# Dilated attention with paired heads on the two column halves, and a last product by token tiles, in a two-block decoder on one core

## What is computed

```python
# dilated attention, per query block and head slot h, groups g = 0..2 with their own keys
sc = q_g @ k_g.T * scale                    # masked to t - dil*j
p_g, den_g = exp(sc - m), sum(exp(sc - m))
o_g = (p_g @ v_g) / den_g
w = softmax over g of (m_g + log(den_g))    # so that sum_g w_g o_g = sum_g p_g v_g / sum_g den_g
y_a = sum_g(w_g * o_g) @ w_proj_a
mixed = sigmoid(gate_a) * y_a + sigmoid(gate_b) * y_b
x = x + mixed @ w_out

# end of the second block, last layer
y = square(relu(h @ w1)) @ w2
x = x + y * rsqrt(mean(y * y) + eps) * g[5]      # this x is the output
```

## Time and profile before

| | us |
|---|---|
| median of 3 runs | 1407.98 |
| the profiled execution's own time | 1406.7 |
| its span, first to last instruction | 1404.9 |
| TensorE busy | 1382.0 (98%) |
| VectorE busy | 1012.8 (72%) |
| ScalarE busy | 741.0 (53%) |
| POOL busy | 80.7 (6%) |
| mean granted TensorE clock | 0.998 |

### The profile page before, as it was taken

One profiled execution on the slowest core, in us unless ns is written; L12 is line 12 of the kernel. 1 busy time (PEld: TensorE's weight loads), 2 busy tenths in 40 slices (PEclk: granted clock), 3 DMA queues, 4 the chain that ended last, 5 costly groups with the idle time before them and its releaser, 6 DMA issues.

```text
span 1404.9 us, 20190 instructions
## 1 busy us (share of the span) xinstructions
PE 1382.0 (98%) x7868; PEld 1179.3 (84%) x7868; DVE 1012.8 (72%) x1529; ACT 741.0 (53%) x1136; POOL 80.7 (6%) x90
## 2 busy tenths in 40 slices
PE   8999999999999999999999999999999999999997
PEld 6899888888888997888888778888888878888886
DVE  5565678777764657977787776887676866886665
ACT  4564555455445554555555666654445664554443
POOL 0000001000000000211111001000000000100000
PEclk9999999999999999999999999999999999999999
DMA  9744355555565334656655424358866523355551
GB/s 304 242 139 151 121 180 195 195 180 182 178 209 180 121 120 153 219 191 206 208 198 159 152 90 132 124 195 225 218 191 207 168 88 117 115 191 197 192 198 71
DMA packets 154437, 242.31 MB, mean 172 GB/s; under 512 B 4523, under 2 KB 107067, under 8 KB 154078
## 3 DMA queue, kind: packets, MB, share of 16 engines
q1 hardware_dynamic: 150626, 227.23, 49.1%
q0 software_dynamic: 3712, 13.77, 3.6%
q10 hardware_dynamic: 4, 0.01, 0.0%
HBM read 239.03 MB, written 1.97 MB: 172 GB/s over the span
## 4 chain that ended last, share of the span: by engine, by line
PE 93%; DVE 4%; ACT 1%; issue 1%; DMA 0%; POOL 0%; SPq 0%; DVEq 0%; ACTq 0%
PE ps L953 19%; PE ps L919 17%; PE ps L926 16%; PE ps L923 16%; PE ps L956 10%; PE ps L1031 3%; PE ps L1119 3%; PE ps L1085 2%; PE ps L1100 1%; DVE wlo L2129 1%; PE ps L993 1%; PE ps L995 1%; PE ps L994 1%; DVE x L2563 0%; PE ps L1572 0%
## 5 line engine op out<-in xcount | busy, mean ns | idle before, releaser
L2129 DVE TENSOR_TENSOR wlo<-raw,whi 128x1024 fp32r<-128x1024 f32 (+1 forms) x432 | 538.6, 1258 | 197.2 <-ACT whi L1659 196.6
L1659 ACT CAST whi<-raw 128x1024 fp32r<-128x1024 f32 (+1 forms) x432 | 446.5, 1042 | 272.3 <-PE ps L926 174.3
L953 PE MATMUL ps<-act,whi 128*128 128x512 f32 x1184 | 324.9, 395 | 1.2 <-DVE wlo L2129 0.9
L919 PE MATMUL ps<-whi,mhi 128*128 128x512 f32 (+2 forms) x688 | 236.4, 393 | 1.9 <-DVE mlo L2156 1.9
L953 PEld LDWEIGHTS ps<-act,whi 128*128 128x128 f32 x1184 | 204.8, 189 | 31.9 <-DVE wlo L2129 1.6
L926 PE MATMUL ps<-whi,mlo 128*128 128x512 f32 (+2 forms) x688 | 231.4, 385 | 0.0
L923 PE MATMUL ps<-wlo,mhi 128*128 128x512 f32 (+2 forms) x688 | 231.1, 385 | 0.0
L956 PEld LDWEIGHTS ps<-act,wlo 128*128 128x128 f32 x1184 | 182.6, 189 | 25.7
L956 PE MATMUL ps<-act,wlo 128*128 128x256 f32 x1184 | 189.4, 281 | 0.0
L919 PE MATMUL ps<-whi,act 128*128 128x256 f32 (+1 forms) x512 | 169.2, 331 | 0.0
L923 PE MATMUL ps<-wlo,act 128*128 128x256 f32 (+1 forms) x512 | 165.2, 323 | 0.0
(11 more groups left out here) (269 smaller groups left out, 1471.8 us busy)
## 6 DMA issues: line engine op xcount, KB each, us to landing
raw<-in_mlp_w SPq DMA_DIRECT2D x64, 1024.0 KB, 5.3
raw<-in_w_up SPq DMA_DIRECT2D x44, 1024.0 KB, 5.1
raw<-in_w_in SPq DMA_DIRECT2D x39, 1024.0 KB, 5.1
raw<-in_w_down SPq DMA_DIRECT2D x22, 1024.0 KB, 4.9
raw<-in_ev_w_in SPq DMA_DIRECT2D x10, 1024.0 KB, 5.4
raw<-in_w_out SPq DMA_DIRECT2D x8, 1024.0 KB, 5.0
raw<-in_xa_wkv SPq DMA_DIRECT2D x4, 1024.0 KB, 5.3
raw<-in_ev_w_out SPq DMA_DIRECT2D x4, 1024.0 KB, 5.1
```

The lines of the kernel that those rows point to most:

```text
L919: nc.tensor.matmul(o, hi[:, kx, rows_], wh[:, k, c0:c0 + w], start=first and h == 0 and k == 0 and (tt == 0 or at[1] == 0), stop=False)
L953: nc.tensor.matmul(both, wh[:, k, w], act2[:, kx].rearrange("p i n -> p (i n)"), start=kx == 0, stop=False)
L1659: nc.scalar.copy(whi[:, m % HL, 0:w], raw[:, n % RAW, h * w:h * w + w]).then_inc(hi_done, 1)
L2129: nc.vector.tensor_tensor(wlo[:, m % HL, 0:w], raw[:, n % RAW, h * w:h * w + w], whi[:, m % HL, 0:w].bitcast(F32), ALU.subtract).then_inc( ...
```

## The change

For the dilated heads:

- `values` gives way to `column_values`: two units (heads h and h + 1 of one query tile) at a time; the values are stationary, 128x64, and the turned exponents move, 128 columns; the two heads write partitions 0 to 63 and 64 to 127 of bank 6, blocks of the two heads in turn. The result lies with head dimensions on the partitions and queries along the row, as the projection wants it. The values of a pair (j, j + 1) stand at step j + 4.
- The copy of a unit waits until the values of the pair before its own pair are done.
- The sums belong to queries, which now lie along the row. VectorE takes all 8 reciprocals at once, POOL spreads each over the 64 columns of its head (`spread_shares`), TensorE turns that (`turn_shares`, between the two halves of "pb"), ScalarE copies it to SBUF, and VectorE multiplies bank 6 by it. ScalarE takes the high half of the product and VectorE the low one, both from SBUF. The turning in the middle of "pb" is gone.
- In ScalarE's program the copy of the turned shares stands ahead of the sigmoids.

For the end: the last chunk is done by token tiles (`tile_chunk`), and squares, mean, root, gain and addition follow tile by tile; tile 0 is added in one operation of 128x1024 and stored at once, tile 1 in two halves, each stored when ready.

The operations are those of `column_values`, `turn_shares` and the copies first (the first `u0 + j - j % 2` stands in ScalarE's program and in the same form in VectorE's), then the two sequences at the end of the attention, then `tile_chunk` and `last_tiles` for the end.

```diff
+            def spread_shares(l):
+                pool.wait_ge(share_ready, l + 1)
+                nc.gpsimd.tensor_copy(spread.rearrange("p (t h d) -> p t h d", t=TT, h=HG), rden[:, :, 0:HG].unsqueeze(3).to_broadcast([P, TT, HG, HD])
+                                      ).then_inc(spread_ready, 1)
...
+                def column_values(i):
+
+                    pair = [(u0 + i + j, us[i + j]) for j in range(2)]
+                    for u, _ in pair:
+                        wait_copied(pe, u)
+                    n = len(us[i]["pv"])
+                    for b in range(n):
+                        for u, d in pair:
+                            row = half(d["slot"])
+                            mm = nc.tensor.matmul(ps[row:row + HD, d["o_bank"], d["o_col"]:d["o_col"] + P], d["pv"][b],
+                                                  values_of(u, d)[:, b * P:(b + 1) * P], start=b == 0, stop=b == n - 1)
+                    mm.then_inc(at_o, 2)
...
-                        if WIDE_LAG + 1 <= i:
-                            values(i - WIDE_LAG - 1)
+                        j = i - WIDE_LAG - 2
+                        if j >= 0 and j % 2 == 0:
+                            values(j)
...
+                def turn_shares():
+                    bank = group_bank(("y1", l, "a"))
+                    pe.wait_ge(spread_ready, l + 1)
+                    wait_copied(pe, first_unit["dil", l] + len(units_of["dil", l]) - 1)
+                    for b in range(2):
+                        for qt in range(TT):
+                            mm = nc.tensor.transpose(bank[:, SEQ * b + P * qt:SEQ * b + P * qt + P], spread[:, SEQ * qt + P * b:SEQ * qt + P * b + P], ident)
+                    mm.then_inc(pe_grp, 1)
...
-                                   middle=attended if h else None)
+                        half_chunk(plan.jobs["pb", l][0], h, mhi, mlo, 2, [[(0, 512, yb(tt, 0)), (512, 512, yb(tt, 1))] for tt in range(TT)], True, True)
+                        if h == 0:
+                            turn_shares()
...
-                pe.wait_ge(grp_dve, plan.by_number[plan.groups["y1", l, "a"]][2])
+                pe.wait_ge(attended_lo, l + 1)
...
-                            if u0 + j >= 2:
-                                act.wait_ge(at_o, u0 + j - 1)
+                            if u0 + j - j % 2:
+                                act.wait_ge(at_o, u0 + j - j % 2)
...
+                take(("y1", l, "a"), shares)
                 act.wait_ge(gate_pre, 2 * NGC * (l + 1))
                 for c0 in (D, 0):
                     nc.scalar.activation(gates[:, :, c0:c0 + D], gates[:, :, c0:c0 + D], ACT.Sigmoid).then_inc(gate_done, 1)
                 split_half(f0 + 2 * NGC + 4)
-                take(("y1", l, "a"), blocks(mhi, 0))
+                act.wait_ge(o_ready, o_counts["dil", l])
+                nc.scalar.copy(blocks(mhi, 0), attended).then_inc(attended_hi, 1)
...
+                    if after and i == len(units_of["dil", l]) + 1:
+                        dve.wait_ge(at_e, first_unit["dil", l] + len(units_of["dil", l]))
+                        nc.vector.reciprocal(rden[:, :, 0:HG], den[:, :, 0:HG]).then_inc(share_ready, 1)
                     if i % 2 == 0 and i:
                         gate_out(3 + i // 2)
                     split_half(f0 + 10 + i)
...
-                for qt in range(TT):
-                    norm_out(("dil", l), HG * qt, HG, heads_of(o_nat, qt, 0, HG), TT * HG)
+                dve.wait_ge(at_o, first_unit["dil", l] + len(units_of["dil", l]))
+                dve.wait_ge(grp_act, plan.by_number[plan.groups["y1", l, "a"]][1])
+                nc.vector.tensor_tensor(attended, ps[:, 6, :], shares, ALU.mult).then_inc(o_ready, 2)
...
                 gate_b(0, 0)
-                lo_of(("y1", l, "a"), mhi, mlo, 0)
+                dve.wait_ge(attended_hi, l + 1)
+                nc.vector.tensor_tensor(blocks(mlo, 0), attended, blocks(mhi, 0).bitcast(F32), ALU.subtract).then_inc(attended_lo, 1)
...
+            def tile_chunk(n, hi, lo, k0, bank):
+                for tt in range(TT):
+                    for c in range(2):
+                        o = ps[:, bank(tt, c), :]
+                        for h in range(2):
+            ...
+                            nc.tensor.matmul(o, xh, wh, start=False, stop=False)
+                            nc.tensor.matmul(o, xh, wl, start=False, stop=False)
+                            mm = nc.tensor.matmul(o, xl, wh, start=False, stop=h == 1)
...
+                gain(0, 0)
+                mean(0)
+                n = gain(0, 1)
+...
+                add(0, slice(0, D)).then_inc(x_ready, 1)
+                gain(1, 0)
+                mean(1)
+                n = gain(1, 1)
+...
+                for c in range(2):
+                    add(1, slice(512 * c, 512 * c + 512)).then_inc(x_ready, 1)
```

More of the change, by code:

```diff
@@ L657, in build_network @@
             rs_count[k] = total
+        attended, spread, shares = o_nat[:, 0, 0:512], o_nat[:, 1, 0:512], o_nat[:, 0, 512:1024]
         def sbk(h):
@@ L890, in _ @@
                             root((key, l), 2, True, ss[:, i, tt:tt + 1], rstd[:, i, tt:tt + 1])
+                    elif key == "ym" and l == DEPTH - 1:
+                        i = NORM[key, l]
+                        for tt in range(TT):
+                            root((key, l), 2, True, ss[:, i, tt:tt + 1], rstd[:, i, tt:tt + 1])
+                        break
                     else:
@@ L1132, in values_pair @@
                         values(i + 1)
-                return scores, turn_pair if not wide_units else turn, values_pair if not wide_units else values
+                return scores, turn_pair if not wide_units else turn, values_pair if not wide_units else column_values
             def attention(key, each=None):
@@ L1876, in _, with squares @@
                 split_half(n0 + 4)
-            def squares(job, key, l, banks=yb, cs=(0, 1)):
+            def squares(job, key, l, banks=yb, cs=(0, 1), tiles=range(TT)):
                 i = NORM[key, l]
                 for c in cs:
-                    for tt in range(TT):
+                    for tt in tiles:
                         product(job(c), tt, c)
@@ L2100, in _ @@
                     memory_hi(l + 1, n0)
-                squares(lambda c: ("w2", l, NMB - 1), "ym", l)
+                if l + 1 < DEPTH:
+                    squares(lambda c: ("w2", l, NMB - 1), "ym", l)
+                else:
+                    for tt in range(TT):
+                        squares(lambda c: ("w2", l, NMB - 1), "ym", l, tiles=(tt,))
         @block.vector
@@ L2582, in add_normed, with last_tiles, gain, mean @@
                 add(1)
+                dve.wait_ge(x_ready, x_count(key, l))
+            def last_tiles(key, l, job):
+                n_gain[0] += 1
+                n_sq[0] += 4
+                i = NORM[key, l]
+                dve.wait_ge(gainb_in, 16 * n_gain[0])
+                def gain(tt, c):
+                    product(job, tt, c)
+                    dve.wait_ge(ss_ready, n_sq[0] - 3 + 2 * tt + c)
+                    cs = slice(512 * c, 512 * c + 512)
+                    return mark(nc.vector.tensor_tensor(ystep[:, tt, cs], ps[:, yb(tt, c), :], gain_b[:, cs], ALU.mult))
+                def mean(tt):
+                    dve.wait_ge(ss_ready, n_sq[0] - 2 + 2 * tt)
+                    total = ss[:, i, tt:tt + 1]
+                    nc.vector.scalar_tensor_tensor(out=total, in0=total, scalar=EPS2, in1=ss[:, i, TT + tt:TT + tt + 1],
+                                                   op0=ALU.add, op1=ALU.add).then_inc(mean_ready, 1)
+                def add(tt, cs):
+                    return nc.vector.scalar_tensor_tensor(out=x[:, tt, cs], in0=ystep[:, tt, cs], scalar=rstd[:, i, tt:tt + 1],
+                                                          in1=x[:, tt, cs], op0=ALU.mult, op1=ALU.add)
+                gain(0, 0)
+                mean(0)
+                n = gain(0, 1)
+                dve.wait_ge(rstd_ready, rs_count[key, l])
+                after(n)
+                add(0, slice(0, D)).then_inc(x_ready, 1)
+                gain(1, 0)
+                mean(1)
+                n = gain(1, 1)
+                dve.wait_ge(rstd_ready, rs_count[key, l] + 1)
+                after(n)
+                for c in range(2):
+                    add(1, slice(512 * c, 512 * c + 512)).then_inc(x_ready, 1)
                 dve.wait_ge(x_ready, x_count(key, l))
```

49 lines of the change are left out of this document (36 added, 13 removed).

## The result

| | before | after |
|---|---|---|
| median, us | 1407.74 (6 runs, 1406.99 to 1407.98) | 1413.89 (6 runs, 1410.99 to 1415.03) |
| after / before | | 1.0039, 95% interval 1.0028 to 1.0050 |
| profiled execution, us | 1406.7 | 1412.05 |
| its span, us | 1404.9 | 1410.2 |
| mean granted TensorE clock | 0.998 | 0.997 |

The change makes the kernel slower by 0.4%. The forecast was 1410.2 with the range 1406.0 to 1414.0: the time lies in the range, at its upper end. (The mean counts the idle end of the program too: the 0.998 of before is nothing but its end, where the clock falls behind the last product.)

The account below looks back on a forecast made before the run. TensorE, busy for 98% of the span, was taken as the bound. Two layers at +2.2 us less 2.2 at the end gave +2.2 on 1406.7, 1408.9; the median being 1.3 higher, 1410.2, range 1406.0 to 1414.0.

Parts of the forecast that it names:

- part 1: Dilated attention, values in pairs on column halves: 2.0 us saved per layer up to the mark, bounds 1.7 to 2.3.
- the mark: Moment in the dilated attention where the turning of the seventh unit ends; "pa" started 10.7 us behind it before.
- part 2: From the mark to the turned shares: a bare VectorE copy, shares turned 6.7 to 7.4 us behind the mark, 7.0 taken.
- rival C: POOL's copy spreading the shares is slow throughout, 3.41 us: +1.6 us a layer, 1413.5; chance 0.08.
- part 3: ScalarE's order: 7.9 us from turned shares to "pa", TensorE standing still 3.5 us a layer, "pa" 4.2 later.
- part 4: End of the program, last chunk by token tiles: 2.2 us gained, bounds 1.4 to 2.9.
- rival B: TensorE's clock falls at the standstill before "pa", costing 1.7 us per layer: 1411.9 once, 1413.6 twice; chance 0.22.
- D: TensorE's own 4.4 us behind the turned shares, not ScalarE, sets the start of "pa": 1402.6; chance 0.09.
- E: Column halves in the values don't overlap, pairs cost 1.3 and 2.6 us: +2.6 us a layer, 1415.4; chance 0.03.

Follow-up runs that it names:

- head_by_head: The sigmoids_first kernel with all blocks of one head of a pair computed before those of the other, instead of in turn: 1407.45 us, ratio 0.9998.
- sigmoids_first: The changed kernel with the two sigmoids put back ahead of ScalarE's copy of the turned shares: 1403.66 us, ratio 0.9974.
- split_sigmoid: sigmoids_first with only the first-needed sigmoid ahead of the shares, the other and next high half behind the high part, VectorE's low part before its gate products: 1402.06 us.
- tail_only: The kernel before the change with only the new end added, the old attention kept: 1404.83 us, ratio 0.9982.
- spares: The changed kernel with twelve unused TensorE products on the identity, into a free bank, in the standstill before "pa": 1409.53 us, ratio 1.0013.
- heads_only: The changed kernel with the old end put back, so the attention's part of the change alone: 1414.98 us, ratio 1.0050.
- pair_schedule: The kernel before, its old form of the values kept but placed where the pairs stand, copies waiting for the pair: 1410.90 us, ratio 1.0024.

## Why the prediction was right, and where it was wrong

**Right: part 1.** A pair of small units takes 0.66 + 0.15 and one of large units 1.33 + 0.15 (0.81 and 1.48 in the chain), as worked out from the earlier trace rows. From the first scores to the mark layer 0 takes 26.81 us against 28.86: 2.05 saved, forecast 2.0. head_by_head shows the condition that the earlier trace rows met and the prediction did not mention: alternate blocks. In part that is luck: the prediction priced the form and not the order.

**Right: part 2.** Bare copy of 0.97, shares turned at 155.21, mark + 6.87, forecast 7.0. Between its two ends (copy by POOL hidden, 6.7, or held, 7.4) the hidden one holds; its own terms, 6.2 for the first half of "pb" and 0.7 for the turning, make 6.9 and not 6.7. POOL's timeline:

```profile
152.97 1.49 POOL L817 COPY o_nat<-rden 128x512 f32<-128x512 f32 x1 [108.31 <-DVE rden L2468]
```

It ends at 154.46, before the first half of "pb" does (154.63). VectorE's low half ran beside it from 152.81 to 153.99, and the copy was not held back until then; it is 0.45 longer than the 1.04 of the multiplication in the earlier trace rows and far from its 3.41, so rival C falls too. The Trainium skill (GPSIMD Engine Reference, Specifications) has POOL contend with VectorE for SBUF. The trace shows a copy that is slower than that multiplication while a VectorE operation with two SBUF inputs runs; whether the neighbour or the kind of operation makes the 0.45, no run here separates. What the prediction drew from the page, the end at 7.4, did not come.

**Right: part 3.** From the turned shares to "pa" 7.87 us, forecast 7.9; standstill 3.49, forecast 3.5; "pa" at mark + 14.74, forecast 14.9. sigmoids_first shows that the order of ScalarE's queue makes 2.6 us of the standstill (0.9 left); the rest goes in split_sigmoid, where the second sigmoid and the next high half, and on VectorE a gate product, leave the way too. The table load took 1.28 and the sigmoids began 1.30 behind its start (155.84 and 157.14), now on the path. The Trainium skill (ScalarE: Activation LUTs, What ACT_TABLE_LOAD costs) would add a drain of 1.38; in this place, too, the trace has none.

**Right: part 4.** 2.3 us in the traces, 2.6 in tail_only, forecast 2.2 with bounds to 2.9. The store of 256 KB landed after 2.1 us, the value taken. The addition and the root fell by 1.33 (2.74 to 1.41) and 0.16.

**Wrong: the weight of rival B.** The sum of the parts is +2.2 us, and with the clock held up it is what the chip gives: spares has +2.1 by the medians. But the likeliest case left out that the clock falls. The time lies inside the range because the range reached up to B, not because the sum of 1410.2 was near. The step that failed is the argument against B, that the fall need not come at a distance of 2.8 us as in the earlier trace rows, and that a stop ringed by full work might be spared. It came in both layers, and in both layers of heads_only too; in spares and sigmoids_first it came in neither. Three of the six runs of after show a lower mean clock than the profiled one. B's mechanism held, and its price came out: forecast 1.7 a layer and 1413.6 for twice, measured 1.6 a layer and a median of 1413.89. The price is luck in part: it took the low level to last as long as the stop, and pair_schedule shows the same 3.4 us of low clock with no stop before it. The chances should have been the other way round: the one row that showed the clock behind a standstill showed a fall, and no row read for it showed a stop of that length without one.

**The other rivals.** D needs the table load and the sigmoids to be off the path. They are not in after, and split_sigmoid, which takes them off, starts "pa" within 0.2 us of D's place (11.3 with 6.9 for the shares in D's sum); its time, 1402.06, is near D's 1402.6. E asked for pairs of 1.3 and 2.6 us; in after they take 0.81 and 1.48.

## What to carry to other kernels

When an operation is put at the head of an in-order queue, count everything behind it, not the operation: here a copy of 0.6 us, put ahead of a table load and two sigmoids (4.9 us), cost 10 us by the medians, wait and clock together, and put behind the first sigmoid, with the second moved behind the high part and VectorE's low part moved ahead, it turned the same change from 0.4% slower to 0.4% faster. Where a change makes TensorE stand still as long as here, 3.5 us, between stretches of full work, put a price on the clock as well as on the wait, take the case with the fall as the likely one, and look for it in the products behind the gap, not in the gap. Two heads on two column halves pay in full only if their blocks alternate. Before a difference of 1 or 2 us is laid to an edit, compare the granted clock along the two profiled executions.

## What the runs showed of the hardware that was not expected

The clock fell when TensorE was already at work again. The last product of "pb" ends at 159.59, "pa" starts at 163.08 at 1.00, and 0.50 begins at 163.6; in layer 1 these are 528.17, 531.66 and 532.3. So full work behind the gap did not prevent the fall. With twelve spare products in the gap the clock stayed at 1.00, and so it did behind gaps of 0.9 us (sigmoids_first) and of 1.2 us (the bare copy). Gaps between 1.2 and 3.5 us were not tried.

A gap is not needed for a fall: in three of ten profiled executions the clock went to 0.50 near 26.5 us for 3.4 us, behind work without a wait above 0.1 us. What sets that off no run here shows.

Two column halves driven one head after the other still cost less than double (2.40 against 1.48 us for 24 records), and a little less than the old form (2.64). The records don't tell what overlaps there.
